# Expert matrices loaded as pairs, and a gate matrix laid out by four keys

## What is computed

```python
# per token: 8 heads x 16 chosen experts, with softmax gates
h = x . u[expert]                 # one dot product of 1024 per chosen expert
a = gelu(h) * gate
y = sum over chosen experts of a * v[expert]
out = layer_norm(alpha * x1 + y)
```

## Time and profile before

| | |
|---|---|
| median of 3 runs | 3060.47 us (3056.7 to 3060.66) |
| the profiled execution | 3062.79 us, its span 3061.1 us |
| TensorE busy / VectorE busy | 2617.2 us (85%) / 2307.9 us (75%) |
| ScalarE busy / GpSimd busy | 1049.6 us (34%) / 1620.0 us (53%) |
| DMA moved | 833.44 MB, mean 272 GB/s |
| mean granted clock of TensorE | 0.938 |

### The profile page before, as it was taken

One profiled execution on the slowest core, in us unless ns is written; L12 is line 12 of the kernel. 1 busy time (PEld: TensorE's weight loads), 2 busy tenths in 40 slices (PEclk: granted clock), 3 DMA queues, 4 the chain that ended last, 5 costly groups with the idle time before them and its releaser, 6 DMA issues.

```text
span 3061.1 us, 40460 instructions
## 1 busy us (share of the span) xinstructions
PE 2617.2 (85%) x14808; PEld 2033.3 (66%) x14808; DVE 2307.9 (75%) x4894; ACT 1049.6 (34%) x1649; POOL 1620.0 (53%) x1187
## 2 busy tenths in 40 slices
PE   7998788889996565644678999999999999999996
PEld 5886676778775565542445767777767777677775
DVE  4512667657999899965777778777778777789999
ACT  4412334333544676751112222322222322222322
POOL 0010011024887555545666666677666767766774
PEclk9999899999998787876889999999999999999999
DMA  4323222131111799999999999999999999999995
GB/s 129 127 81 118 85 87 87 45 119 52 58 59 36 260 300 309 322 296 373 379 383 387 391 386 382 401 394 397 387 394 376 408 404 409 391 382 347 366 377 209
DMA packets 309808, 833.44 MB, mean 272 GB/s; under 512 B 26128, under 2 KB 114640, under 8 KB 309616
## 3 DMA queue, kind: packets, MB, share of 16 engines
q0 software_dynamic: 150864, 548.60, 46.7%
q1 hardware_dynamic: 158752, 282.31, 26.1%
HBM read 771.93 MB, written 58.88 MB: 271 GB/s over the span
## 4 chain that ended last, share of the span: by engine, by line
PE 18%; DVE 12%; DMA 12%; POOL 8%; issue 5%; ACT 0%; SPq 0%; DVEq 0%; ACTq 0%; POOLq 0%
DMA e_u_row<-in_u,ids 11%; POOL hold L2081 5%; DVE e_u_row L2319 3%; PE psum L2157 3%; PE psum L2124 3%; PE psum L2158 3%; PE psum L2159 3%; PE psum L2125 3%; PE psum L2126 2%; PE psum L2172 2%; POOL e_u_row L2072 2%; DVE e_y L2309 2%; DVE e_u_row L2328 1%; DVE e_vl L2277 1%; DVE hold L2328 1%
## 5 line engine op out<-in xcount | busy, mean ns | idle before, releaser
L2072 POOL DMA_INDIRECT e_u_row<-in_u,ids x384 | 485.6, 1265 | 330.3 <-DVE ids L2319 236.3
L2319 DVE CUSTOM_DVE_ANT_0 e_u_row<-e_u_row,hold 128x1024 f32<-128x1024 f32 x384 | 468.3, 1224 | 242.6 <-DMA e_u_row<-in_u,ids 242.0
L2157 PE MATMUL psum<-e_vh,e_ah 128*128 128x512 f32 x1024 | 420.7, 411 | 102.1 <-DVE e_y L2309 82.6
L2081 POOL DMA_INDIRECT hold<-in_v,ids x376 | 435.5, 1158 | 134.4 <-issue 108.8
L2158 PE MATMUL psum<-e_vl,e_ah 128*128 128x512 f32 x1024 | 409.2, 400 | 0.0
L2159 PE MATMUL psum<-e_vh,e_al 128*128 128x512 f32 x1024 | 407.4, 398 | 0.0
L2124 PE MATMUL psum<-x1d,e_uh 128*128 128x512 f32 x864 | 341.0, 395 | 0.0
L2125 PE MATMUL psum<-x1d,e_uh 128*128 128x512 f32 x864 | 337.2, 390 | 0.0
L2157 PEld LDWEIGHTS psum<-e_vh,e_ah 128*128 128x128 f32 x1024 | 198.1, 193 | 209.2 <-DVE e_y L2309 109.9
L2126 PE MATMUL psum<-x1d,e_ul 128*128 128x512 f32 x864 | 336.3, 389 | 0.0
L2309 DVE TENSOR_TENSOR e_y<-e_y,psum 128x512 f32<-128x512 f32 x464 | 299.7, 681 | 13.1 <-PE psum L2159 13.1
(11 more groups left out here) (407 smaller groups left out, 5628.9 us busy)
## 6 DMA issues: line engine op xcount, KB each, us to landing
e_vr<-in_v SPq DMA_DIRECT2D x128, 512.0 KB, 6.7
e_ur<-in_uT SPq DMA_DIRECT2D x108, 512.0 KB, 7.2
s_G<-g_tile SPq DMA_DIRECT2D x8, 4096.0 KB, 27.0
e_g<-s_G SPq DMA_DIRECT2D x64, 512.0 KB, 9.0
ids<-in_w_ch SPq DMA_DIRECT2D x17, 512.0 KB, 4.1
s_ch<-p_out POOLq DMA_DIRECT2D x16, 512.0 KB, 3.3
hold<-in_wq SPq DMA_DIRECT2D x16, 512.0 KB, 4.4
hold<-in_v,ids POOLq DMA_INDIRECT x476, 8.7
```

Of the source, the lines that this page charges most:

```text
L2072: pool.indirect_dma_start(out=u_ring[n % U_RING][:], out_offset=None, in_=io["u"], in_offset=bass.IndirectOffsetOnAxis(ap=id_u[:, s, k:k + ...
L2081: pool.indirect_dma_start(out=v_ring[m % V_RING], out_offset=None, in_=io["v"], in_offset=bass.IndirectOffsetOnAxis(ap=id_v[:, t:t + 1], a ...
L2157: nc.tensor.matmul(acc, ah[s][j][:, r], vh[s][j][:, c], start=(first and j == 0), stop=False)
L2319: nc.vector.tensor_tensor_reduce(row, row, xs[:, s, :], 1.0, 0.0, ALU.mult, ALU.add, hs[:, s, k:k + 1]).then_inc(dotted, 1)
```

## The change

Four edits, which share a tile of gates:

1. U's two blocks of a group are one transfer of 1 MB with 8 KB in a row for each partition, into one tile `u_raw` (the host lays U out so). It waits for both halves of the group before. The first dense group still loads two halves.
2. V's two blocks are one such transfer, into `v_raw[g % 2]`, two tiles which have the same memory as `vl`, so the low part is written over the loaded one. It waits until `values(g - 2)` are done. `split_v(g, 0)` moves, on VectorE behind `dots 7` and on ScalarE behind the work of both j.
3. The gates come for two groups at once (KEYS_G = 4 first keys, 1 MB with 8 KB in a row), in every second group, into the one tile `gt`, which is twice as big. The stores of the matrix have runs of 1 KB and not 512 B. PSUM's banks hold four tokens interleaved: each 128x128 product is written to every fourth float, and the evacuation reads a bank in order and writes runs of four floats. R_ACT is 7.
4. PHASE[1] is 19 and not 18.

```diff
-PHASE = (0, 18, 36, 53, 64)
+PHASE = (0, 19, 36, 53, 64)
@@ build_gates
-        R_ACT = 5
+        R_ACT = 7
-                        last = nc.tensor.matmul(psum[:, n // 4, (n % 4) * NK:(n % 4 + 1) * NK],
+                        last = nc.tensor.matmul(psum[:, n // 4, :].rearrange("p (k t) -> p t k", t=4)[:, n % 4, :],
                                                 one2[s][:, n, :], one1[s][:, n, :], start=True, stop=True)
-                            nc.scalar.activation(gt[b % 2][:, :, r * R + 4 * n:r * R + 4 * n + 4].rearrange("p k t -> p t k"),
-                                                 psum[:, n, :].rearrange("p (t k) -> p t k", t=4),
+                            nc.scalar.activation(gt[b % 2][:, :, r * R + 4 * n:r * R + 4 * n + 4],
+                                                 psum[:, n, :].rearrange("p (k t) -> p k t", t=4),
                                                  ACT.Copy).then_inc(evac[n], 1)
-                             gt[b % 2].rearrange("p (g j) t -> p g (j t)", j=2)).then_inc(stored[b % 2], 16)
+                             gt[b % 2].rearrange("p (g j) t -> p g (j t)", j=KEYS_G)).then_inc(stored[b % 2], 16)
@@ experts: tiles
+        u_raw = sb("e_ur", [P, 2, KC, P])
+        ur = [u_raw[:, j] for j in range(2)]
+        with ExitStack() as below:
+            v_raw = [below.enter_context(nc.sbuf_tensor(f"e_vr{s}", [P, 2, D], F32)) for s in range(2)]
+        v_low = [sb(f"e_vl{s}", [P, 2, D], F32R) for s in range(2)]
+        vl = [[v_low[s][:, j, :] for j in range(2)] for s in range(2)]
-        gt = sb("e_g", [P, TD // TG, 2, TG])
+        gt = sb("e_g", [P, TD // TG, KEYS_G, TG])
@@ experts: SP's queue
+                def load_u(g):
+                    for j in range(2):
                         sp.wait_ge(u_lo[j], g - SHORT)
-                        sp.dma_start(ur[j][:], io["uT"][2 * g + j]).then_inc(u_in[j], 16)
+                    sp.dma_start(u_raw[:], io["uT"][g]).then_inc(pair_in, 16)
                 def load_gates(g):
                     for j in range(2):
                         sp.wait_ge(a_mul[j], g)
-                    sp.dma_start(gt[:], scr["G"][g]).then_inc(g_in, 16)
-                def load_v(g, j):
-                    sp.wait_ge(v_lo[1 - j], g + j)
-                    sp.dma_start(vr[:], io["v"][(2 * g + j) * NK:(2 * g + j + 1) * NK, :]).then_inc(v_in[j], 16)
+                    sp.dma_start(gt[:], scr["G"][2 * g // KEYS_G]).then_inc(g_in, 16)
+                def load_v(g):
+                    if g >= 2:
+                        sp.wait_ge(y_mm, Q * (g - 1))
+                    sp.dma_start(v_raw[g % 2][:], io["v2"][g]).then_inc(v_in[g % 2], 16)
                 for g in range(NG):
                     if SHORT < g + 1 < NG:
-                        for j in range(2):
-                            load_u(g + 1, j)
-                    load_gates(g)
-                    load_v(g, 0)
-                    if g + 1 <= SHORT:
-                        for j in range(2):
-                            load_u(g + 1, j)
-                    load_v(g, 1)
+                        load_u(g + 1)
+                    if 2 * g % KEYS_G == 0:
+                        load_gates(g)
+                    load_v(g)
+                    if g + 1 < SHORT:
+                        load_activated(g + 1)
+                    elif g + 1 == SHORT:
+                        load_first_u()
@@ experts: VectorE's order
                     dot_rows(g, 3)
-                    split_v(g, 0)
                     weigh(g, 1)
...
                     dot_rows(g, 7)
+                    split_v(g, 0)
                     if g:
                         gather(g - 1, 6, Q)
                     split_v(g, 1)
```

More of the change, by code:

```diff
@@ L38 @@
 TG = 64
+KEYS_G = 4
 ALPHA = 2.0 ** 0.25
@@ L100, in ts, with u_block @@
     return bass.ds(start, size)
+def u_block(io, b):
+    return io["uT"][b // 2][:, b % 2]
 def wait_apart(engine, tick, semaphore, value):
@@ L1268, in load_u @@
                 sp.wait_ge(u_lo, b)
-                sp.dma_start(ur[:], io["uT"][b]).then_inc(u_in, 16)
+                sp.dma_start(ur[:], u_block(io, b)).then_inc(u_in, 16)
             def store_hidden(b):
@@ L1941, in experts @@
         y = sb("e_y", [P, ND, D])
-        ur = [sb(f"e_ur{j}", [P, KC, P]) for j in range(2)]
-        vr = sb("e_vr", [P, D])
+        u_raw = sb("e_ur", [P, 2, KC, P])
+        ur = [u_raw[:, j] for j in range(2)]
         uh = [sb(f"e_uh{j}", [P, KC, P], F32R) for j in range(2)]
@@ L1960, in experts @@
         lng, lnb = (ur[j].rearrange("p k e -> p (k e)") for j in range(2))
-        ln_in = 16 * (NG + 1)
+        ln_in = 16 * (SHORT + 2)
         u_in = [sem(f"u_in{j}") for j in range(2)]
-        v_in = [sem(f"v_in{j}") for j in range(2)]
+        pair_in = sem("u_pair_in")
+        v_in = [sem(f"v_in{s}") for s in range(2)]
         g_in = sem("g_in")
@@ L2025, in load_u, with load_first_u @@
                                      scr["hidden"][2 * g + j]).then_inc(u_in[j], 16)
-                    else:
+                def load_first_u():
+                    for j in range(2):
                         sp.wait_ge(a_mul[j], SHORT)
+                        sp.dma_start(ur[j], io["uT"][SHORT][:, j]).then_inc(u_in[j], 16)
+                def load_u(g):
+                    for j in range(2):
                         sp.wait_ge(u_lo[j], g - SHORT)
-                        sp.dma_start(ur[j][:], io["uT"][2 * g + j]).then_inc(u_in[j], 16)
+                    sp.dma_start(u_raw[:], io["uT"][g]).then_inc(pair_in, 16)
                 def load_gates(g):
@@ L2033, in load_gates @@
                         sp.wait_ge(a_mul[j], g)
-                    sp.dma_start(gt[:], scr["G"][g]).then_inc(g_in, 16)
-                def load_v(g, j):
-                    sp.wait_ge(v_lo[1 - j], g + j)
-                    sp.dma_start(vr[:], io["v"][(2 * g + j) * NK:(2 * g + j + 1) * NK, :]).then_inc(v_in[j], 16)
-                for j in range(2):
-                    load_u(0, j)
+                    sp.dma_start(gt[:], scr["G"][2 * g // KEYS_G]).then_inc(g_in, 16)
[3 more added lines that the diff above has]
+                    sp.dma_start(v_raw[g % 2][:], io["v2"][g]).then_inc(v_in[g % 2], 16)
+                load_activated(0)
                 for g in range(NG):
                     if SHORT < g + 1 < NG:
-                        for j in range(2):
-                            load_u(g + 1, j)
-                    load_gates(g)
-                    load_v(g, 0)
-                    if g + 1 <= SHORT:
-                        for j in range(2):
-                            load_u(g + 1, j)
-                    load_v(g, 1)
+                        load_u(g + 1)
[6 more added lines that the diff above has]
+                        load_first_u()
                     if g == 0:
@@ L2197, in split_u @@
                 def split_u(g, j):
-                    act.wait_ge(u_in[j], 16 * (g + 1))
+                    if g > SHORT:
+                        act.wait_ge(pair_in, 16 * (g - SHORT))
+                    else:
+                        act.wait_ge(u_in[j], 16 * (SHORT + 1))
                     act.wait_ge(h_mm[j], g - SHORT)
@@ L2570, in layout @@
         "wq": blocks(a["peer_wq"][0]), "keysT": np.ascontiguousarray(keys),
-        "uT": np.ascontiguousarray(a["peer_u"][0].reshape(NK, NK, KC, P).transpose(0, 3, 2, 1)),
-        "u": a["peer_u"][0], "v": a["peer_v"][0], "ln2_g": a["ln2_g"][0], "ln2_b": a["ln2_b"][0],
+        "uT": np.ascontiguousarray(a["peer_u"][0].reshape(NK // 2, 2, NK, KC, P).transpose(0, 4, 1, 3, 2)),
+        "u": a["peer_u"][0], "v": a["peer_v"][0],
+        "v2": np.ascontiguousarray(a["peer_v"][0].reshape(NK // 2, 2, NK, D).transpose(0, 2, 1, 3)), "ln2_g": a["ln2_g"][0], "ln2_b": a["ln2_b"][0],
         "consts": constants(), "wmask": window_masks(),
```

18 lines of the change are left out of this document (8 added, 10 removed).

## The result

The changed kernel takes 3090.07 us in the median (3087.28 to 3096.31, 4 runs) against 3058.74 in the same session: a ratio of 1.0096, 95% interval 1.0082 to 1.0109. It is slower, where I forecast 16 us less. The profiled execution's span is 3089.0 us.

What follows compares the result with a forecast made beforehand. VectorE paced the gate stage, DMA groups 0 to 9, TensorE from 1865 us (DMA full too), VectorE the last rows. Terms -6 + 0 - 16 + 6 = -16 us gave 3044.5 from 3060.47; predicted 3046, range 3030 to 3078.

Steps and rivals of the forecast that it cites:

- Dense loads as pairs: Expert stage: gates late in the last stretch, +6 us (other end +19); middle groups 0, far end +42.
- First phase one group longer: Expert stage: fewer gathered bytes a group, groups 0 to 9 -11, 10 to 17 -6, +1 elsewhere: -16 us.
- Gate stage: Rows moved from VectorE to ScalarE: 17.0 us less, 10.7 us lost to longer waits for uh: -6 us.
- Storing and entering: Gate matrix stores and next stage's first loads: -1.5 us for longer runs, +1.4 for the bigger gate load, together 0.
- (a): Expert stage: gates late through even sharing, TensorE pays in the middle too; +18 to +39 us, about 3083; chance 0.17.
- (b): Gate stage: matmuls into every fourth float of PSUM run slower, +19 us, giving 3063; chance 0.13.
- (c): Expert stage's short groups aren't bound by bytes: -3 us in sum, 3057; chance 0.10.

Runs made afterwards that it cites:

- gswap: The changed kernel with the gates leaving just before U's pair, at the same moment, not just behind it: 3092.47 us, ratio 1.0099.
- keys2: The changed kernel with the gates of one group at a time (512 KB, KEYS_G = 2): 3072.37 us, ratio 1.0048.
- gfirst: The changed kernel with the gates ahead of U's pair in SyncE's queue, with their own wait alone: 3076.28 us, ratio 1.0056.
- uhalves: The changed kernel with U loaded in two halves, each as soon as its own half is split: 3079.36 us, ratio 1.0063.
- ubunch: vpair with both halves of U waiting for both splits and leaving together, still as two transfers: 3084.18 us, ratio 1.0085.
- vpair: The changed kernel with U in two halves, each after its own split, PHASE[1] = 18 and KEYS_G = 2: 3060.36 us, ratio 1.0016.
- bphase19: The kernel before with PHASE[1] = 19 alone: 3069.01 us, ratio 1.0029.
- uhalves18: The changed kernel with U in two halves, each after its own split, and PHASE[1] = 18: 3074.93 us, ratio 1.0049.
- phase18: The changed kernel with PHASE[1] back at 18: 3079.74 us, ratio 1.0076.
- rows4k: The changed kernel with the three dense transfers issued at the same points, but with rows of 4 KB: 3093.95 us, ratio 1.0108.
- vlate: The changed kernel with V's pair held back behind VectorE's split of U's next first half: 3103.47 us, ratio 1.0147.
- gates7: The kernel before with the gate stage's edits alone (7 rows on ScalarE, interleaved banks, runs of four floats): 3054.75 us, ratio 0.9986.

## Why the prediction was wrong, step by step

**The step that failed: "Dense loads as pairs ... I take 0; the far end is 21 x 2".** I priced one consequence, whether the gates land in time. That price was good where it was the right question: late 6.0 us in four even groups of the last stretch, which lost 4.7 us (predicted +6). In the middle, where I took 0, the groups 18 to 52 lost 31 us. The gates were late there too (14.1 us over the even groups of 19 to 53), but gswap took that away and the middle still took 26.9 us a group. What costs there is when, and in what portions, the dense transfers leave. The DMA engines were at share 1.00 before; I had read that as "the DMA engines full as well", and not as a second bound with nothing to spare. keys2, gfirst, uhalves and ubunch each change only when or in what portions the same bytes go, and move the median by 18, 14, 11 and 24 us. V as a pair, which I had also booked at 0, cost the middle nothing: vpair has it, at 26.0 us a group. By windows the changed kernel moved 391 and 381 GB/s in 1882 to 2340 and 2340 to 2792, at shares of 0.99 and 0.98, for 392 and 394 at 1.00.

```profile
1882.00:2340.00 458.00, 446.62 (x2158) 320.89 (x2157) 354.66 (x537) 113.83 (x174) 317.44 (x257) 0.99 0.99 391
2340.00:2792.00 452.00, 439.02 (x2132) 314.98 (x2131) 344.96 (x520) 113.63 (x174) 298.85 (x246) 1.00 0.98 381
```

What VectorE and TensorE wait for in groups 19 to 52 of each trace (sums in us; "rows of U" and "gates" are VectorE's waits for landings, "adds" is TensorE's wait for VectorE's adds of y):

| | us a group | rows of U | gates | adds |
|---|---|---|---|---|
| before | 25.9 | 137.9 | 2.1 | 4.9 |
| vpair | 26.0 | 138.6 | 0.0 | 5.0 |
| bphase19 | 26.2 | 156.3 | 2.5 | 11.3 |
| gfirst | 26.3 | 170.6 | 0.0 | 15.1 |
| keys2 | 26.4 | 152.3 | 2.1 | 14.8 |
| uhalves18 | 26.4 | 152.7 | 0.0 | 12.6 |
| phase18 | 26.4 | 154.4 | 7.0 | 15.2 |
| ubunch | 26.5 | 141.4 | 31.6 | 18.3 |
| uhalves | 26.5 | 166.0 | 0.3 | 18.2 |
| changed | 26.8 | 163.6 | 14.1 | 23.0 |
| rows4k | 26.8 | 142.7 | 36.3 | 24.3 |
| gswap | 26.9 | 177.2 | 0.0 | 27.2 |
| vlate | 27.1 | 176.3 | 5.7 | 23.5 |

My reading: while SyncE's queue sends a bunch, something in it or beside it comes late. With 8 KB rows the gathers get a third of the engines and rows of U are late; with 4 KB rows they get a half and the gates are late; with the gates ahead, the rows of U again. VectorE stands either way, its adds of y come late, and TensorE waits for a bank. In the table the last column goes with the time of a group, nearly in order, whichever of the two waits feeds it. Once the bunch is over, the gathers, on rings of 4 and 8 rows, are all that fills the engines, and at 2054.5 us they don't. In stretches of 2 us from group 19 to 52, 31 of 440 moved under 350 GB/s before and 59 of 454 after. That a dry ring makes these dips is read from such moments; no experiment deepened a ring. gfirst and vlate don't keep the order of the table exactly.

**"First phase one group longer": -16.** Wrong in two places. I let the short groups' time follow their bytes. Groups 0 to 9 gave 6.9 us for 11 here, but bphase19 shows that the edit alone gives nothing in groups 0 to 18: the bytes fell, and the rate fell with them. Groups 0 to 9 took 254.7 to 262.6 us in the eight traces with PHASE[1] = 19 and 256.0 to 261.6 us in the nine with 18, so the 6.9 us are scatter. And "the third phase, which already has 17 groups" isn't the second's density: its dots run to 52.75, 17.75 groups long, so it has 15.0 rows a group where the new second phase has 15.3. Over the stretches the traces count 15.1 gathers a group in 19 to 35 of bphase19 and 14.5 in 36 to 52. The former take 26.4 us for 26.0, at 399 GB/s. The term measured some +10 (bphase19: 1.3 to 4.5 per mille) and not -16.

**Gate stage: -6.** Right that a wait would eat most of VectorE's 17.0 us. In the changed kernel's trace the steps took as long as before; over the twelve traces with this gate stage and ScalarE's old order they took 327.7 to 335.1 us, 332.2 in the mean, for 334.7 and 335.8 in the two with the old stage. So it gained some 3 us, not 6. The wait for uh rose by 6.8 and not 10.7 us, and that for gathered rows by 6.9, which I hadn't priced; in gates7 they rose by 8.4 and not at all, so how the rest splits is not shown.

**Storing and entering.** From the last store to the first load of the next stage 19.1 us before, 21.8 after (1352.31 to 1374.15): the stretch grew where I had -1.5. But that is the gate stage's doing (gates7, with the old stores, has 22.9): with its last store issued 3 us sooner behind the last `one1`, more of the storing is left; from that `one1` to the first load it is 28.8 us for 29.2. Among the kernels with this gate stage and ScalarE's old order, last store to first load is 21.5 to 23.1 us in the four with runs of 512 B and 20.2 to 22.0 us in the eight with runs of 1 KB, so the longer runs gave some 1 us, near what I had said. From the first load to the first weighing it is 14.3 us for 12.8, for the +1.4 of the bigger load.

**The rivals.** (a), gates late, had the right engines. I summed it wrongly: +18 to +39 around 3060.47 has its middle at 3089, not 3083, so its size was that of the result. That is in part luck, since its mechanism, even sharing and late gates, is not what ran: with 8 KB rows the shares are two to one, and taking the lateness away (gswap) gave nothing back in the middle. Its wait of TensorE for VectorE's adds did come. (b) fell: 170.0 us of products for 172.8. The Trainium skill (Advanced Engine Details and Errata, Memory Cachelines) says that a non-contiguous pattern in PSUM slows matmuls significantly; these, 16 B apart, weren't slowed. Its 16-byte lines of SBUF agree with 0.58 us for an evacuation in runs of four. (c) was right that the short groups aren't bound by bytes; its 3057 left out the middle. My range was too narrow as well: the bounds of the terms themselves (gate stage -3, short groups -3, gates +6) already reach 3060, not 3056.

On the packets, the Trainium skill (DMA: Bandwidth & Descriptors, Queues, rings and completion order) says that a whole packet is drained before the engine switches, and the trace agrees: shares of 66.6 and 34.6% with 8 KB against 4 KB packets, 51.4 and 51.3% with 4 KB in both. But rows4k shows that neither way of sharing saves the time.

## What to carry to other kernels

Where the DMA share is 1.00 beside a busy TensorE, ask of an edit not only whether each transfer still lands in time, but whether the engines have work from every queue throughout: a transfer twice as large that waits for two releases leaves later and in a bunch, and here it cost more than its packets saved (U's pair and the gates' pair; V's pair, with one release and a point of its own, cost the middle nothing). Removing the wait that the profile shows may only move it to the next load of the bunch. Before moving work off the engine that sets the pace, look at the order on the engine that receives it: what the first waits for must stand ahead of the new work. A density argument needs the count of the rows themselves (here, where each `spread` ends), not the length of the phase.

## What was unexpected of the hardware

An 8 KB packet takes about as long as two of 4 KB (medians of 309 and 160 ns in the changed kernel's trace, groups 19 to 52), so larger rows gain little, but they give the queue that has them two thirds of the engines and not a half. And the dip to 215 GB/s at 2054 us isn't made by 8 KB packets: rows4k has it at the same place with 4 KB ones, and the kernel before has a smaller one, at a moment when its SyncE queue has nothing in flight (windows of rows4k, then of before):

```profile
2054.00:2056.00 2.00, 1.58 (x8) 1.28 (x8) 2.00 (x3) 0.00 (x0) 1.56 (x2) 1.00 0.74 240
```
```profile
2046.00:2048.00 2.00, 2.00 (x11) 1.65 (x10) 2.00 (x3) 0.00 (x0) 1.70 (x2) 1.00 0.78 248
```

A share of 1.00 over hundreds of us hides such moments; windows of 2 us show them.
